# Attention by head: probabilities turned in 32x32 blocks on VectorE, value products in four row tiles, sums from a ones column

## The reference

```python
q = (rmsnorm(cq, q_norm) @ w_uq)   # 8 heads x 96 (64 plain, 32 with rope), scaled
kv = (rmsnorm(ckv, kv_norm) @ w_ukv)   # 8 heads x (64 key + 64 value), rope key shared
s = jnp.einsum('bqhd,bkhd->bhqk', qblk, k)
p = jax.nn.softmax(s, axis=-1)
o = jnp.einsum('bhqk,bkhd->bqhd', p, v)   # 512 x 8 x 64
a = rmsnorm(o, att_out_norm)
mix = jnp.concatenate([a, r], axis=-1) @ w_o   # r: the recurrence, gated and normed
```

## Time and profile before

| what | us |
|---|---|
| median of 3 runs | 1365.39 |
| the profiled execution, its own time | 1366.18 |
| its span in the trace | 1364.4 |
| TensorE matmul busy in the span | 1324.7 (97%) |
| VectorE busy | 883.2 (65%) |
| ScalarE busy | 672.1 (49%) |
| GpSimd busy | 670.4 (49%) |

### The profile page before, as it was taken

How to read it: one execution, slowest core, us unless ns; L and a number is a source line. 1 busy time by engine, 2 the same in 40 slices (tenths; PEclk the granted TensorE clock), 3 DMA queues, 4 the chain that set the end, 5 groups by cost and what they waited for, 6 DMA issues and landing times.

```text
span 1364.4 us, 22084 instructions
## 1 busy us (share of the span) xinstructions
PE 1324.7 (97%) x8300; PEld 1081.2 (79%) x8300; DVE 883.2 (65%) x1182; ACT 672.1 (49%) x1245; POOL 670.4 (49%) x536
## 2 busy tenths in 40 slices
PE   6999999999989999999999999999999999999997
PEld 5887878877857777888888888888888888878886
DVE  7126566545886775166755565657899888895384
ACT  6233333344458775356755545454544444445452
POOL 3365545365447744455577777775100552003490
PEclk9999999999999999999999999999999999999999
DMA  6221111112240004443533434337677735674251
GB/s 208 70 70 40 32 43 30 36 35 69 55 101 2 1 1 142 168 132 123 193 116 114 126 108 125 110 122 245 226 217 246 242 106 145 231 248 140 86 187 68
DMA packets 138265, 162.28 MB, mean 119 GB/s; under 512 B 16688, under 2 KB 82224, under 8 KB 138160
## 3 DMA queue, kind: packets, MB, share of 16 engines
q1 hardware_dynamic: 138160, 160.87, 38.1%
HBM read 139.86 MB, written 18.87 MB: 116 GB/s over the span
## 4 chain that ended last, share of the span: by engine, by line
PE 84%; DVE 8%; issue 3%; POOL 2%; ACT 2%; DMA 1%; SPq 0%; DVEq 0%; POOLq 0%; ACTq 0%
PE ps L51 25%; PE ps L53 24%; PE ps L52 24%; PE ps L1878 2%; PE ps L1919 2%; PE ps L1040 2%; PE ps L1690 2%; DVE lat_low L809 1%; DVE op_low L2356 1%; DVE wy_low L2362 1%; PE ps L1073 1%; PE ps L1088 1%; PE ps L987 1%; DVE w_sum L2333 0%; POOL k_low L1707 0%
## 5 line engine op out<-in xcount | busy, mean ns | idle before, releaser
L1590 POOL TENSOR_TENSOR wy_low<-w_raw,wy_high 128x512 fp32r<-128x512 f32 x107 | 159.4, 1492 | 178.7 <-ACT wy_high L1533 178.6
L51 PE MATMUL ps<-wy_high,op_high 128*128 128x512 f32 x448 | 175.0, 391 | 1.3 <-DVE wy_low L2362 0.9
L53 PE MATMUL ps<-wy_high,op_low 128*128 128x512 f32 x448 | 174.3, 389 | 0.0
L52 PE MATMUL ps<-wy_low,op_high 128*128 128x512 f32 x448 | 174.3, 389 | 0.0
L1533 ACT ACTIVATE wy_high<-w_raw 128x512 fp32r<-128x512 f32 x118 | 74.4, 631 | 153.4 <-PE ps L53 149.2
L399 POOL TENSOR_TENSOR wx_low<-w_raw,wx_high 128x512 fp32r<-128x512 f32 x62 | 81.8, 1324 | 127.4 <-ACT wx_high L519 127.4
L1590 POOL TENSOR_TENSOR wy_low<-t_sum,wy_high 128x512 fp32r<-128x512 f32 x64 | 89.3, 1395 | 54.0 <-ACT wy_high L1533 54.0
L1533 ACT ACTIVATE wy_high<-w_sum 128x512 fp32r<-128x512 f32 x80 | 50.6, 632 | 119.4 <-PE ps L53 96.6
L1590 POOL TENSOR_TENSOR wy_low<-w_sum,wy_high 128x512 fp32r<-128x512 f32 x32 | 44.4, 1387 | 130.4 <-ACT wy_high L1533 130.4
L51 PE MATMUL ps<-a_high,wy_high 128*128 128x512 f32 x256 | 100.1, 391 | 0.0
L51 PEld LDWEIGHTS ps<-wy_high,op_high 128*128 128x128 f32 x448 | 84.1, 188 | 19.8 <-DVE wy_low L2362 1.7
(11 more groups left out here) (298 smaller groups left out, 3441.9 us busy)
## 6 DMA issues: line engine op xcount, KB each, us to landing
w_raw<-in_w_down SPq DMA_DIRECT2D x127, 256.0 KB, 3.4
raw_more<-in_w_down SPq DMA_DIRECT2D x65, 256.0 KB, 3.6
w_raw<-in_w_up SPq DMA_DIRECT2D x64, 256.0 KB, 3.3
w_raw<-in_w_in SPq DMA_DIRECT2D x62, 256.0 KB, 2.8
w_raw<-in_w_o SPq DMA_DIRECT2D x32, 256.0 KB, 2.9
raw_more<-in_w_up SPq DMA_DIRECT2D x32, 256.0 KB, 3.4
w_raw<-in_w_ple_gate SPq DMA_DIRECT2D x32, 256.0 KB, 2.8
keep_h<-comb SPq DMA_DIRECT2D x26, 256.0 KB, 2.5
```

Source lines behind the costliest of these rows:

```text
L51: pe.matmul(out, stat_high, mov_high, start=start, stop=False)
L52: pe.matmul(out, stat_high, mov_low, start=False, stop=False)
L53: return pe.matmul(out, stat_low, mov_high, start=False, stop=stop)
L1590: pool.tensor_tensor(low_tile, tile_raw(tile), high_tile.bitcast(F32), ALU.subtract).then_inc(low_made, 1)
```

## The change

The work goes by head: a step is now a group g, a head h (together n = 0 to 15, `values_of` calls it n) and a residue r = 0 to 3. A step's 128 queries are every fourth of the head's 512 (`every_fourth`, a stride of 16 bytes in the stationary operand). Score banks are three instead of two. The exponential has no accumulator any more.

The probabilities are turned by VectorE, 16x4 blocks of 32x32 in one instruction, from `prob` to `prob_t`; the output is written with a stride of four elements, so that after four steps 32 keys x 128 queries lie side by side. There are no transposes of probabilities on TensorE and no copies out of PSUM. A block holds 32 keys in one of four partition groups, so a product contracts over 32 rows: `values_of` issues 16 x 4 = 64 products for a head, partition group a to PSUM bank 4 + a, with `prob_t` stationary (32 x 128) and the values of 32 keys moving (65 columns: 64 values and a column of ones, whose result is the sum). The result has queries on partitions, so it isn't turned any more; `read_outputs` inverts four sums and multiplies 4 x 64 columns once per head.

The values must lie in all four partition groups: they are written to DRAM (`keep_v`) and read back four times per pair of heads (`load_rows`, 4 transfers of 256 KB, in pieces of 512 bytes). For that the value jobs stand ahead of the key jobs. Two memsets on VectorE (left out below) write the ones columns. `turn_early` turns half a tile at a time (tiles 0 to 3, steps 44 to 58) through bank 3.

```diff
+HEADS, GROUP = 2 * AH, P // 4
+PAIR_WIDE = 2 * VD + 2
+v_rows = [at(f"v_rows{i}", [P, SEQ // GROUP, PAIR_WIDE], F32, o)
+          for i, o in enumerate((a_at + 22144, a_at, x_at))]
+rows_of_pair = [0, 1, 0, 1, 0, 2, 0, 2]
+turn_of_pair = [rows_of_pair[:i].count(rows_of_pair[i]) for i in range(AH)]
...
+def load_rows(sp, pair):
+    g, first = pair // 4, pair % 4 * 2 * VD
+    source = keep_v[g * SEQ:(g + 1) * SEQ, first:first + 2 * VD].rearrange("(c j) v -> j c v", j=GROUP)
+    for a in range(4):
+        sp.dma_start(v_rows[rows_of_pair[pair]][a * GROUP:(a + 1) * GROUP, :, 1:1 + 2 * VD],
+                     source).then_inc(rows_in[rows_of_pair[pair]], 16)
...
     jobs = [("q_rope", 0, 0), ("q", 0, 0), ("q", 0, 1), ("q_rope", 0, 1), ("q", 1, 0), ("q", 1, 1),
             ("q_rope", 1, 0), ("q", 2, 0), ("q", 2, 1), ("q_rope", 1, 1), ("q", 3, 0), ("q", 3, 1)]
+    jobs += [("v", i, 0) for i in range(TT)]
     jobs += [("k", m, h) for m in range(4) for h in range(2)]
-    jobs += [("v", i, 0) for i in range(TT)]
...
         sp.wait_ge(o_full, 2 * HH)
         for k in range(2):
             sp.dma_start(wkv[:, k, :].rearrange("p (h c) -> p h c", h=AH), ukv[:, :, k, :]).then_inc(wkv_loaded, 16)
-        for m in range(2):
+        def keep_values(g):
+            by_dve, by_act = readers(12 + 4 * g + 3)
+            sp.wait_ge(job_dve, by_dve)
+            sp.wait_ge(job_act, by_act)
+            for i in range(4 * g, 4 * g + 4):
+                sp.dma_start(keep_v[i * P:(i + 1) * P, :], v_att[:, i, :]).then_inc(v_kept, 16)
+
+        def place_queries(m):
             sp.wait_ge(q_roped, 2 * (m + 1))
             for h in range(4):
                 sp.dma_start(q_t[NOPE:QK, 4 * m + h, :],
                              q_rope[h * ROPE:(h + 1) * ROPE, m, :]).then_inc(placed, 16)
-            if m == 0:
...
+
+        keep_values(0)
+        place_queries(0)
+        sp.wait_ge(hg_made, 4 * 2)
+        sp.wait_ge(w_low_made, XTILES)
+        sp.wait_ge(k_roped, 5)
+        for g in range(2):
+            sp.dma_start(k_t4[NOPE:QK, g, :, :],
+                         k_rope[:, HALVES[g]].unsqueeze(1).broadcast_to([ROPE, AH, SEQ])).then_inc(placed, 16)
+        sp.wait_ge(v_kept, 16 * 4)
+        load_rows(sp, 0)
+        place_queries(1)
+        keep_values(1)
         sp.dma_start(gain[:, 0:HH * HK], row(hg_out_norm)).then_inc(gains_in, 16)
         sp.dma_start(gain[:, HH * HK:], row(att_out_norm)).then_inc(gains_in, 16)
...
+    def turn_early(pe, t, part):
+
+        if part == 0:
+            pe.wait_ge(scaled6, t + 1)
+        else:
+            pe.wait_ge(hg_done, t + 1)
+        if t or part:
+            pe.wait_ge(a_split, 2 * t + part)
+        for i in range(4):
+            src = recur[:, t, i, :] if part else att_out[:, t, i * P:(i + 1) * P]
+            last = pe.transpose(ps[:, TURN_BANK, i * P:(i + 1) * P], src, ident[:, :])
+        last.then_inc(done, 1)
...
     def act_attention(act):
-        for s in range(STEPS + 3):
+        for s in range(STEPS):
             t, h = s // AH, s % AH
-            if s < STEPS:
...
+            act.wait_ge(top_made, s + 1)
+            if s >= 2:
+                act.wait_ge(pt_made, s - 1)
+            act.activation(prob[:, s % 2, :], ps[:, s % SBANKS, :], ACT.Exp,
+                           bias=top_neg[:, s % SBANKS:s % SBANKS + 1]).then_inc(p_made, 1)
+            if h == 2:
                 if t:
                     act.wait_ge(hg_summed, t)
                 act.activation(square_hg[:, :], recur[:, t, :, :].rearrange("p h v -> p (h v)"),
                                ACT.Square).then_inc(hg_squared, 1)
-            if h == 5 and 1 <= t < TT:
...
+            if s in (37, 39, 41, 43):
+                norm_square(act, (s - 37) // 2)
+            if s >= 45 and s % 2:
+                if s < 45 + 16:
+                    turned_part(act, 0, (s - 45) // 4, (s - 45) // 2 % 2)
...
     def dve_attention(dve):
-        def read_outputs(t):
...
+        def read_outputs(n):
+
+            g, h, at = n // AH, n % AH, n % 2 * P
+            sums, values = (at + VD, at) if n % 2 else (at, at + 1)
+            dve.wait_ge(pv_done, n + 1)
+            dve.reciprocal(prob_inv[:, n % 2, :].unsqueeze(2), ps[:, 4:8, sums:sums + 1]).then_inc(inverted, 1)
+            dve.wait_ge(inverted, n + 1)
+            dve.tensor_tensor(att_out[:, 4 * g:4 * g + 4, h * VD:(h + 1) * VD], ps[:, 4:8, values:values + VD],
+                              prob_inv[:, n % 2, :].unsqueeze(2).broadcast_to([P, 4, VD]),
                               ALU.mult).then_inc(o_read, 1)
+
+        def turn_blocks(s):
+
+            n = s // 4
+            dve.wait_ge(p_made, s + 1)
+            if n >= 2 and s % 4 == 0:
+                dve.wait_ge(pv_done, n - 1)
+            if s == 4:
+                dve.wait_ge(v_kept, 16 * TT)
+            dve.transpose(prob_t[:, 1 - n % 2, :, :, s % 4], prob[:, s % 2, :].rearrange("p (c j) -> p c j", j=GROUP)).then_inc(pt_made, 1)
...
         dve.wait_ge(gains_in, 32)
-        for s in range(STEPS + 3):
+        for s in range(STEPS + 5):
             t, h = s // AH, s % AH
             if s < STEPS:
                 dve.wait_ge(s_full, s + 1)
-                if s >= 2:
-                    dve.wait_ge(p_made, s - 1)
-                dve.tensor_reduce(top_neg[:, s % 2:s % 2 + 1], ps[:, s % 2, :], AX.X, ALU.max,
+                if s >= SBANKS:
+                    dve.wait_ge(p_made, s - SBANKS + 1)
+                dve.tensor_reduce(top_neg[:, s % SBANKS:s % SBANKS + 1], ps[:, s % SBANKS, :], AX.X, ALU.max,
                                   negate=True).then_inc(top_made, 1)
-            r = s - 2
...
+            if 2 <= s < STEPS + 2:
+                turn_blocks(s - 2)
+            if s >= 8 and s % 4 == 0:
+                read_outputs((s - 8) // 4)
+            if t < TT and h == 3:
+                hgrn_mean(t)
+            if s in (38, 40, 42, 44):
+                norm_mean((s - 38) // 2)
+            if s in (41, 43, 45, 47):
+                norm_scale((s - 41) // 2)
+            if 46 <= s < 46 + 16 and s % 2 == 0:
+                low_half(dve, 0, (s - 46) // 4, (s - 46) // 2 % 2)
+        for t in range(4, TT):
+            norm_mean(t)
+        for t in range(4, TT):
+            norm_scale(t)
+
+    def values_of(pe, n):
+
+        pair, at = n // 2, n % 2 * P
+        rows, cols = v_rows[rows_of_pair[pair]], slice((VD + 1) * (n % 2), (VD + 1) * (n % 2 + 1))
+        pe.wait_ge(pt_made, 4 * n + 4)
+        pe.wait_ge(rows_in[rows_of_pair[pair]], 1 + 64 * (turn_of_pair[pair] + 1))
+        if n >= 2:
+            pe.wait_ge(o_read, n - 1)
+        for c in range(SEQ // GROUP):
+            for a in range(4):
+                of = slice(a * GROUP, (a + 1) * GROUP)
+                last = pe.matmul(ps[:, 4 + a, at:at + VD + 1], prob_t[of, 1 - n % 2, c, :, :].rearrange("p i r -> p (i r)"),
+                                 rows[of, c, cols], start=c == 0, stop=c == SEQ // GROUP - 1)
         last.then_inc(pv_done, 1)
 
-    def outputs_turned(pe, t):
...
     def pe_attention(pe):
-        pe.wait_ge(job_dve, JOBS_DVE - 3)
...
+        pe.wait_ge(placed, 16 * 10)
         for s in range(STEPS + 3):
-            t, h = s // AH, s % AH
...
+            n, r = s // 4, s % 4
+            if s < 3:
+                pe.wait_ge(job_dve, JOBS_DVE - (7, 6, 0)[s])
+                pe.wait_ge(job_act, JOBS_ACT - (7, 6, 0)[s])
             if s < STEPS:
-                if s < 4:
-                    pe.matmul(ps[:, s % 2, :], q_t[:, h, 0:P], k_t4[:, h, 0:SEQ], start=True, stop=True).then_inc(s_full, 1)
+                g, h, bank = n // AH, n % AH, ps[:, s % SBANKS, :]
+                here = slice(g * SEQ, (g + 1) * SEQ)
+                if s >= SBANKS:
+                    pe.wait_ge(p_made, s - SBANKS + 1)
+                if n == 0:
+                    pe.matmul(bank, every_fourth(q_t[:, h, here], r), k_t4[:, g, h, :], start=True,
+                              stop=True).then_inc(s_full, 1)
                 else:
-                    q_part, k_part = ("q", t, h // 4), ("k", t // QT, h)
...
+                    if r == 0:
+                        pe.wait_ge(score_split, score_at["q", n] + 1)
+                    three_passes(pe, bank, every_fourth(q_high[n % 2][:, :], r), every_fourth(q_low[:, h, here], r),
+                                 k_high[n % 2][:, :], k_low[:, g, h, :], True, True).then_inc(s_full, 1)
+            if s >= 6 and r == 2:
+                values_of(pe, n - 1)
+            if 44 <= s < 44 + 16 and s % 2 == 0:
+                turn_early(pe, (s - 44) // 4, (s - 44) // 2 % 2)
...
+        sp.wait_ge(s_full, 1)
+        load_rows(sp, 1)
         for q in range(len(raws)):
             if raws[q] == ("e", first[M2]):
                 sp.wait_ge(sums_kept, 16 * SUMMED)
             if q == 3:
-                sp.wait_ge(o_turned, TT)
+                for pair in range(2, AH):
+                    if pair == 5:
```

(5 more changed lines are left out.)

256 lines of the change are left out of this document (74 added, 182 removed).

## The result

| | before | after |
|---|---|---|
| median of the runs, us | 1365.74 (1365.29 to 1368.87, 4 runs) | 1511.82 (1511.49 to 1512.99, 4 runs) |
| the profiled execution's own span | 1364.4 | 1511.2 |
| mean granted clock of it | 1.00 | 0.913 |

The ratio is 1.1066, with a 95% interval of 1.1046 to 1.1085: slower, as forecast, but by 146 us where 59 were forecast and with the time above the range's 1490.

What follows compares the result with a forecast made beforehand. TensorE was taken to bound the kernel, its matmuls filling 97% of the span. Terms 29.2 + 11 + 13.7 + 2.4 + 1.6 + 1 = 58.9 on 1366.2 gave 1425.1, median 0.8 lower: 1424 us, range 1392 to 1490.

Steps and rivals of the forecast that it cites:

- the chain: Attention, per head: the burst delays score r = 3, then three maxima and block transposes precede the next burst; 9.8 us.
- front, to the first maximum: Kernel start: gains queue behind twelve value transfers and land late, so the first maximum moves to 414; +13.7 us.
- first maximum to first burst: Attention's opening: score parts of the second head, six maxima and transposes take 8.7 us against 6.3; +2.4.
- 15 periods, without the second half: Attention, burst to burst: fifteen periods take 147.0 us where 117.8 stood; +29.2.
- second half: Attention from step 44: half-tile turns wait for VectorE's low part, turns stand behind bursts, plus norm scales; +11 us.
- last burst to projection: End of attention: 3.6 + 0.3 us against 2.3; +1.6.
- behind it: After the projection's start: weight loads wait for four squares, with 8 us of products as cover; +1 us.
- The burst: A head's 64 value products, 128 records: four row tiles load and stream fully beside each other; 3.6 us, bounds 1.9 to 14.3.
- Rival B: Value products come too slowly or only two tiles overlap: burst 7.5 us, total 1487; chance 0.14.
- The period: Attention, one head of 512 queries: 9.8 us instead of 7.6.
- VectorE's stall behind the burst: Attention, each head: VectorE idles on the maximum of r = 3 until TensorE releases it; 3.5 us.
- The block transpose: VectorE's turn of one step's probabilities: 0.65 us, taken from a 32-lane shuffle; bounds 0.3 and 1.3.

Runs made afterwards that it cites:

- experiments 6: experiment 1 with, at steps 2 to 43, two full 512-column products that nobody reads ahead of each burst: 1463.6 us.
- 12: experiments 6 with queries stored in runs (block transposes of 0.70) and two unread full products also ahead of each result turn from step 44 on: 1448.15 us.
- the third experiment: The changed kernel with 16 products of 128 rows per head in place of 64 of 32 rows, leaving out the sum over row groups: 1509.59 us.
- Experiments 5: experiment 1 with, at steps 2 to 43, one full 512-column product that nobody reads behind each score: 1466.73 us.
- experiment 2: The changed kernel with the block transposes writing runs of 32 elements in place of every fourth, so output rows come in another order: 1492.95 us.
- experiment 1: The changed kernel with the front's order put back: queries placed and gains loaded first, value writes and reads behind them: 1499.06 us.
- the tenth: 7 with each value product streaming all 130 columns of its head pair in place of 65: 1414.81 us.
- 7: The changed kernel with experiment 1's front order, each burst in three pieces, and queries stored so block transposes write runs of 32: 1486.55 us.
- 14: 13 with 98 columns per value product in place of 130: 1466.03 us.
- 11: 7 with 16 products of 128 rows per head in place of 64 of 32 rows, leaving out the sum over row groups: 1469.93 us.
- 8: 7 with an unread extra product of 256 columns behind each score of steps 2 to 43: 1502.8 us.
- 15: 14 with one full product behind each score of steps 2 to 5, before the first burst: 1456.2 us.
- 13: the tenth with each burst in four pieces, behind scores r = 2, 3, 0 and 1, and each read ahead of the next r = 2 maximum: 1407.81 us.

## Why the prediction was wrong

The direction was right and so was the chain, but the clock that everything on it was priced at was not, and the size was wrong by 87.8 us. By the prediction's own terms, forecast and measured in the changed kernel:

| term | forecast | measured | from |
|---|---|---|---|
| front, to the first maximum | +13.7 | +17.7 | 418.01 against 400.32 |
| first maximum to first burst | +2.4 | +3.4 | 9.65 us to 427.66 |
| 15 periods, without the second half | +29.2 | +100.5 | 15 x 14.55 = 218.3 against 117.8 |
| second half | +11 | +12.1 | five periods to 657.93 in 84.81, less 5 x 14.55 |
| last burst to projection | +1.6 | +4.7 | 7.04 against 2.30 |
| behind it | +1 | +8.5 | 846.2 against 837.7 |
| sum | 58.9 | 146.9 | span 1511.2 against 1364.4 |

**The burst, "I take full concurrency: 3.6".** Right at 2.4 GHz. There it is 3.80 with its last product's end (rows of experiments 6 and 12), and the third experiment shows four row tiles in the time of one. Rival B's 7.5 was nearly met by 7.10, but for another reason: its products would have been as slow at 2.4 GHz, and they aren't. Of the Trainium skill's 3.07 for four row tiles ("TensorE: Matmul & The Clock Gate", section on measured speedup) nothing shows in these products of 65 columns; by it 4.7 was estimated.

**The period, "9.8".** Right at the clock that the prediction took: 9.66 in experiment 12, whose block transposes take 0.70 and whose fillers stand where TensorE would wait. VectorE's stall behind the burst is there too, 3.60 to 4.06 in its timeline, for 3.5. The chain (burst, score r = 3, three maxima and block transposes) was the right one.

**The granted clock, never a term.** This is the step that failed. The prediction says "at a granted clock of 1.00, the 2.4 GHz level", reads it from the kernel before and carries it over to a stage in which half of TensorE's time goes to other products. At 1.2 GHz the burst takes 7.10 for 3.80 and burst end to the next maximum 1.71 (477.71 to 479.42) for the 1.2 taken, 3.8 in a period, 57 us in 15. Experiments 5 and 6 gave 32 and 35 us of it back in the ten heads that they cover. And no rival had the clock in it.

**The block transpose, "0.65", bounds 0.3 to 1.3.** Mis-sized: 1.09, of which 0.39 is the stride of its output. Three on the chain: (1.09 - 0.65) x 3 x 15 = 20, and experiment 2 gave 18.9 back for 0.39. I had taken the duration of a shuffle that writes in a row, and not looked at how the output lies. The period's rest is 14.55 - 9.8 - 3.8 - 1.3 = -0.35: the forecast's other parts were a little long.

**The front.** The mechanism was right: the gains' landing sets the first maximum in all three kernels. Issue and landing make 394.36 + 5.9 = 400.3 before (first maximum 400.32), 409.05 + 8.9 = 417.95 in the changed kernel (418.01) and 395.65 + 5.9 = 401.55 in experiment 1 (401.56). TensorE's wait of 14.78 for the queries' rope parts ends at 412.51 and costs nothing more, as the prediction said. The 4.0 that are missing are sizes: the four reads of value rows take 5.44 to issue (1.36 each) where 0.61 each was taken, and the last gain takes 8.9 to land, not 5.9; less by quicker issues of the value writes and no wait for them (SyncE goes straight on at 398.38).

**The second half** came out at 12.1 for 11. The turns wait for VectorE's low part at the three places named (4.12, 4.18 and 3.16), but these three periods together are 12.1 longer than the mean of those before, where 6.6 and some 2 for turns behind bursts were forecast, and the last two together aren't longer at all, so the size was part luck. **The end** was short by 3.1, the burst's 3.3 more at 1.2 GHz. **Behind the projection's start** 7.5 are missing. 4.9 are TensorE's one wait that ends with a late load of `w_o`. The squares aren't the cause. The first load behind them is issued at 668.97, as the last square ends, 4.0 behind the projection's start (before: 0.3), and TensorE doesn't pause for it. The late one is issued at 690.86, behind a gain's load for which SyncE's queue has waited 15.7 us, until TensorE's last turn of the attention's output. Before, that wait was 8.0. The change moves the turns of tiles 4 to 7 three weight rows back in TensorE's list (`before = {(0, 4): [(0, 4)], ...` for `{(0, 1): ...`), so the last one starts 25.2 us behind the projection's start, not 14.5. The prediction has no term for that, and no run has the turns put back, so the price of it isn't shown. The low clock has a small share: 0.86 in the first 20 us and 0.91 in the 20 with the wait (1.00 before). In the tenth, at 1.00 in its first 20 us and with a wait of 4.99 there, the stretch still takes 845.0, so most of the 8.5 isn't the attention's clock.

What became of the expected gain, the 1.8 us of transposes and the copies taken off TensorE and the others? Even at 2.4 GHz it doesn't shorten the stage: in the tenth TensorE is busy 85% of 8.94 us, 7.6 a head, which is as long as a head took before. Its pieces take 4.4 (1.40, 1.40, 1.62) where transposes took 1.8 and value products 2.9, with changes of form around them, and the wait for the last block transpose, 1.27, comes on top.

**What stays open.** What exactly holds the clock down. The low clock appears without waits (0.67 a period in 7, none in 14), without products of 32 rows (3, 11) and without the long wait in the front (1), so none of these is needed for it, and the share of busy time doesn't order the runs (14 at 100% is at 0.50, the tenth at 85% at 0.98). The columns that a product streams matter (65 and 130 with one edit between them, 7 and 10), and full products between the bursts can raise it (5, 6) or not (8). Both levels can go on for some 30 us in the same kind of steps (14, 15). Which of this TensorE's clock goes by, no run here says.

## What to carry to other kernels

Before a stage's products are made smaller, look at the granted clock of every stretch as a thing that the change can move: it is worth a rival with a price, here everything that TensorE does on the chain, twice. Busy time doesn't tell: TensorE was 95% busy at either level (7 and 13). If the levels are in doubt, run the kernel once with harmless full products added, or with wider products: where the clock rises, it shows what the rest would take at 2.4 GHz (5, 6 and 10; in 8 it didn't rise). Before taking another instruction's duration, look at the layout that yours writes. And where the profile names an engine that was long done as the one waited for, look for a transfer that landed at that moment.

## What the runs showed of the hardware

- Granted clock 0.50 for 120 us with TensorE 100% busy (14), and 0.98 with it 85% busy (10, 440 to 520). The Trainium skill, "TensorE: Matmul & The Clock Gate", section "Why this matters for your kernels", advises against idle gaps between bursts of matmuls, to avoid drops of the throughput. In these runs a gap isn't needed: by the profile TensorE is never idle for 120 us, and the clock stays low.
- More work made the program faster: products of 130 columns for 65, -71.7 us (10 against 7).
- Four products of 32 rows, 128 wide weights and 65 columns run fully beside each other: 128 records in 7.10 us at 1.2 GHz, against 32 records of all rows in 7.09 at the same clock, and 3.80 at 2.4.
- A block transpose of 128 x 512 numbers of four bytes took 1.09 us where its output lay 16 bytes apart and 0.70 where it lay in runs of 32.
